# Where four small steps stand in a one-core layer kernel: bias split, cached values, row buffer clear, tile order of the last norm

## What is computed

```python
proj = x @ w_in                                   # 256 pool, 3x384 q k v, 768 conv columns
y_pool = pool_mix(u_pool)                         # causal means over 2, 4, 8, 16 rows, minus the row, times pool_w
y_attn = merge_dilations(branches)                # 6 heads x 64, windows (128,1), (512,4), (2048,16)
y_conv = silu(layer_norm(conv31(glu(c_in))))
x = layer_norm(alpha * x + concat(y_pool, y_attn, y_conv) @ w_o)      # first norm
# mixture of experts: 32 experts, top 4 per token
hh = xblk @ e_w_in[e] + e_b_in[e]
gate, up = clip(split(hh))
y = (gate * sigmoid(1.702 * gate) * (up + 1)) @ e_w_out[e] + e_b_out[e]
x = layer_norm(alpha * x + segment_sum(y * gate_of_token))            # final norm
```

## Time and profile before

| what | value |
|---|---|
| median of 3 runs | 1425.38 us (1423.78 to 1426.49) |
| the profiled execution's own time | 1424.93 us |
| its span in the profile | 1422.9 us |
| PE busy | 1228.7 us, 86% |
| DVE, ACT, GpSimd busy | 516.0, 176.7, 322.2 us |
| DMA moved | 463.12 MB, mean 325 GB/s |

### The profile page before, as it was taken

The page is one execution under the profiler, slowest core; times in us unless marked ns, Lnnn a source line. Parts: engine busy times, 40 slices in busy tenths (PEclk is TensorE's granted clock), DMA queues, the critical chain, the costliest instruction groups (busy, mean ns, idle before and its releaser), DMA issues.

```text
span 1422.9 us, 33256 instructions
## 1 busy us (share of the span) xinstructions
PE 1228.7 (86%) x12422; PEld 559.7 (39%) x12423; DVE 516.0 (36%) x822; ACT 176.7 (12%) x350; POOL 322.2 (23%) x266
## 2 busy tenths in 40 slices
PE   6996989996579999999989998998999889996860
PEld 5884454445123334345323343353343323442220
DVE  1996712347342224042222314042222222414225
ACT  0002312212010001011100101011000000101012
POOL 7103011314222121113312131123023212130113
PEclk9997968995689999999999999999999999998885
DMA  9600732026499999999999999999999999999973
GB/s 343 191 3 0 276 111 89 2 118 267 167 413 414 409 410 413 411 406 394 412 417 410 415 407 416 413 408 402 420 415 398 411 419 409 383 403 420 409 277 121
DMA packets 86539, 463.12 MB, mean 325 GB/s; under 512 B 13509, under 2 KB 29610, under 8 KB 36206
## 3 DMA queue, kind: packets, MB, share of 16 engines
q1 hardware_dynamic: 67483, 437.11, 75.5%
q0 software_dynamic: 16672, 18.27, 5.9%
q10 hardware_dynamic: 2354, 7.35, 1.4%
...
## 4 chain that ended last, share of the span: by engine, by line
PE 51%; DMA 17%; issue 3%; DVE 2%; SPq 1%; POOL 0%; POOLq 0%; ACT 0%; DVEq 0%; ACTq 0%
PE pu L1716 32%; PE rest L1730 17%; DMA ring<-in_e_in 9%; DMA ring<-in_e_out 7%; PE pu L1710 1%; SPq L267 1%; PE rest L1741 1%; DVE bn L1896 0%; DVE fin L1912 0%; DMA fin<-acc_rows 0%; DVE xgT L1836 0%; DVE mv L1906 0%; DMA acc_rows<-y,idx 0%; PE rest L1735 0%; DMA xq<-x_rows,idx 0%
## 5 line engine op out<-in xcount | busy, mean ns | idle before, releaser
L1716 PE MATMUL pu<-ring,xgT 128*32 128x512 f32 x5248 | 593.3, 606 | 32.3 <-DMA ring<-in_e_in 31.5
L1716 PEld LDWEIGHTS pu<-ring,xgT 128*32 128x32 f32 x5248 | 167.9, 111 | 440.3 <-issue 439.3
L1730 PE MATMUL rest<-ring,hid 128*32 128x256 f32 x5248 | 296.1, 381 | 19.9 <-DMA ring<-in_e_out 12.3
L1644 POOL DMA_INDIRECT acc_rows<-y,idx x82 | 130.2, 1588 | 758.0 <-ACT y L1784 729.0
L1866 DVE TENSOR_SCALAR gg<-pu 128x1280 f32<-128x1280 f32 x32 | 47.7, 1492 | 608.8 <-PE pu L1716 600.3
L1730 PEld LDWEIGHTS rest<-ring,hid 128*32 128x32 f32 x5248 | 173.2, 110 | 133.0 <-issue 36.1
L1776 ACT ACTIVATE ss<-gg 128x1280 f32<-128x1280 f32 x32 | 40.7, 1271 | 669.6 <-DVE gg L1866 669.6
L825 PE MATMUL pair<-xt,ring 128*128 128x260 f32 x448 | 100.6, 388 | 12.4 <-DMA ring<-in_w_in 12.4
L1635 POOL DMA_INDIRECT xq<-x_rows,idx x82 | 86.2, 1051 | 50.3 <-issue 45.5
L825 PEld LDWEIGHTS pair<-xt,ring 128*128 128x128 f32 x448 | 86.3, 193 | 25.6 <-DMA ring<-in_w_in 12.1
L1784 ACT ACTIVATE y<-rest,gate 128x256 f32 x160 | 61.9, 479 | 250.9 <-PE rest L1730 250.9
(11 more groups left out here) (260 smaller groups left out, 666.5 us busy)
## 6 DMA issues: line engine op xcount, KB each, us to landing
ring<-in_e_in SPq DMA_DIRECT2D x256, 1024.0 KB
ring<-in_e_out SPq DMA_DIRECT2D x128, 1024.0 KB
...
ring<-in_w_in SPq DMA_DIRECT2D x6, 512.0 KB, 12.1
...
```

The source lines that it names most:

```text
L1644: nc.gpsimd.indirect_dma_start(out=acc_quarters, out_offset=bass.IndirectOffsetOnAxis(ap=idx4[:, u % AHEAD, j:j + 1], axis=0), in_=y[:, u ...
L1716: mm = nc.tensor.matmul(pu[quarter(c), j], xgT[:, j, k], w[:, :, c * QC:(c + 1) * QC], start=False, stop=k == KT - 1, skip_group_check=True)
L1730: mm = nc.tensor.matmul(py[quarter(c), j], hid[:, j, 2 * q + f], w[:, f, c * QC:(c + 1) * QC], start=False, stop=q == FT // 2 - 1 and f == ...
```

## The change

Four edits, each of which puts work at another place or on another engine:

1. The out bias is no longer split by GpSimd ahead of the attention but behind its 24 scaling steps. Its rows are loaded by SyncE into the part of `qkv` that held the queries, once the last score product is done (`qk_done`), instead of by GpSimd into `btok`.
2. SyncE issues the cached values ahead of the last out weights and the two norm vectors.
3. GpSimd no longer clears `xq` ahead of the first gather. ACT clears half 0 (ones times zero), and the first gather waits for that; GpSimd clears half 1 between the gathers of jobs 0 and 1.
4. The final norm takes the tiles in the order 4, 0, 1, 2, 3. SyncE issues all five loads in that order. The addition of l2b for the last one (tile 3) is done by DVE.

```diff
@@ -66,6 +66,7 @@
...
 UNITS = 12
+LAST_TILES = (4, 0, 1, 2, 3)
 PAD0 = R + 4
...
@@ -543,23 +544,26 @@
...
             stepped(sp, f"v{NT}")
-            sp.dma_start(flat[:, wo0 + (NPART - 1) * D:wo0 + (KT - 1) * D].rearrange("p (k n) -> p k n", n=D), w_o[:, NPART:]
-                         ).then_inc(ld["wo2"], 16)
-            sp.dma_start(l1g, o["ln1_g"].partition_broadcast(P)).then_inc(ld["l1"], 16)
-            sp.dma_start(l1b, o["ln1_b"].partition_broadcast(P)).then_inc(ld["l1"], 16)
             sp.wait_ge(scored, 1)
...
                              ).then_inc(ld["vc"], 16)
+            sp.dma_start(flat[:, wo0 + (NPART - 1) * D:wo0 + (KT - 1) * D].rearrange("p (k n) -> p k n", n=D), w_o[:, NPART:]
+                         ).then_inc(ld["wo2"], 16)
+            sp.dma_start(l1g, o["ln1_g"].partition_broadcast(P)).then_inc(ld["l1"], 16)
+            sp.dma_start(l1b, o["ln1_b"].partition_broadcast(P)).then_inc(ld["l1"], 16)
             sp.wait_ge(sn_done, 1)
...
                 load_unit(sp, 0, j)
+            sp.wait_ge(qk_done, nsteps)
+            for part in range(3):
+                sp.dma_start(qkv[part * NE:(part + 1) * NE, 0:D], o["e_bout"][0]).then_inc(ld["bout"], 16)
             stepped(sp, "pv2")
...
@@ -609,23 +613,6 @@
...
             keep_high(2 * NE, 3 * NE)
-            for part in range(3):
-                gp.dma_start(btok[part * NE:(part + 1) * NE, 0:D], o["e_bout"][0]).then_inc(ld["bout"], 16)
-            sp_ch.do(nc.gpsimd.memset(drow[:, :], 0.0))
-            gp.wait_ge(ld["bout"], 48)
-            gp.wait_ge(conv_done, 1)
-            def keep_high_out(lo, hi):
-                sp_ch.do(nc.gpsimd.tensor_copy(drow[lo:hi], btok[lo:hi, 0:D]))
-            def take_off_out(lo, hi):
-                sp_ch.do(nc.gpsimd.tensor_tensor(btok[lo:hi, 0:D], btok[lo:hi, 0:D], drow[lo:hi], ALU.subtract))
-            keep_high_out(0, 3 * NE)
-            for part in (1, 2):
-                take_off_out(part * NE, (part + 1) * NE)
-                keep_high_out(part * NE, (part + 1) * NE)
-            take_off_out(2 * NE, 3 * NE)
-            keep_high_out(2 * NE, 3 * NE)
             gp.sem_inc(brow_ready, 1)
...
@@ -648,6 +635,22 @@
...
                     list_rows(NT, 1)
+            otok = qkv[:, 0:D]
+            gp.wait_ge(ld["bout"], 48)
+            gp.wait_ge(listed, 16 * TOPK)
+            def keep_high_out(lo, hi):
+                sp_ch.do(nc.gpsimd.tensor_copy(drow[lo:hi], otok[lo:hi]))
+            def take_off_out(lo, hi):
+                sp_ch.do(nc.gpsimd.tensor_tensor(otok[lo:hi], otok[lo:hi], drow[lo:hi], ALU.subtract))
+            sp_ch.do(nc.gpsimd.memset(drow[:, :], 0.0))
+            keep_high_out(0, 3 * NE)
+            for part in (1, 2):
+                take_off_out(part * NE, (part + 1) * NE)
+                keep_high_out(part * NE, (part + 1) * NE)
+            take_off_out(2 * NE, 3 * NE)
+            keep_high_out(2 * NE, 3 * NE)
             for i in range(NT):
...
@@ -1603,18 +1608,19 @@
...
             sp.wait_ge(sums_done, 1)
-            for i in (0, 2, 4):
+            for i in LAST_TILES:
                 load_sums(sp, i)
-            for i in range(NT + 1):
-                sp.wait_ge(y_ready, i + 1)
+            for n, i in enumerate(LAST_TILES):
+                if n < NT:
+                    sp.wait_ge(y_ready, n + 1)
+                else:
+                    sp.wait_ge(last_ready, 1)
                 dst = o["y_prompt"][0, i * P:(i + 1) * P] if i < NT else o["y_sample"][:, 0]
...
         def _(gp):
-            nc.gpsimd.memset(xq[:, :, :, :], 0.0).then_inc(xq_zero, 1)
-            gp.wait_ge(xq_zero, 1)
 
...
@@ -1651,6 +1657,11 @@
...
                 gp.wait_ge(named, u + 1)
+                if u == 0:
+                    gp.wait_ge(xq_zero, 1)
+                if u == 1:
+                    nc.gpsimd.memset(xq[:, 1], 0.0).then_inc(xq_half_zero, 1)
+                    gp.wait_ge(xq_half_zero, 1)
                 if u >= 1:
...
@@ -1686,9 +1697,9 @@
...
             gp.sem_inc(sums_done, 1)
-            for i in range(NT + 1):
+            for n, i in enumerate(LAST_TILES[:-1]):
                 m = rows(i)
-                gp.wait_ge(scaled2, i + 1)
+                gp.wait_ge(scaled2, n + 1)
                 nc.gpsimd.tensor_tensor(fin[0:m, i], fin[0:m, i], l2b[0:m], ALU.add).then_inc(y_ready, 1)
...
@@ -1785,6 +1796,9 @@
...
 
+            nc.scalar.activation(xq[:, 0].rearrange("p j n -> p (j n)").rearrange("p (a n) -> p a n", n=P),
+                                 C("ones").unsqueeze(1).broadcast_to([P, JG * QC // P, P]), ACT.Copy, scale=0.0
+                                 ).then_inc(xq_zero, 1)
             a.sem_inc(y_done, 2)
...
@@ -1796,20 +1810,19 @@
...
 
-            def ln2_root(i):
-                a.wait_ge(var2, i + 1)
+            def ln2_root(n):
+                i = LAST_TILES[n]
+                a.wait_ge(var2, n + 1)
                 nc.scalar.activation(mv2[0:rows(i), i, 3:4], mv2[0:rows(i), i, 1:2], ACT.Sqrt).then_inc(rstd2, 1)
-            a.wait_ge(sums_done, 1)
-            for i in (1, 3):
-                load_sums(a, i)
-            for i in range(NT + 2):
-                if i <= NT:
-                    ln2_root(i)
-                if i >= 1:
-                    m = rows(i - 1)
-                    a.wait_ge(shift2, i)
-                    nc.scalar.activation(fin[0:m, i - 1], fin[0:m, i - 1], ACT.Identity, bias=mv2[0:m, i - 1, 4:5],
-                                         scale=mv2[0:m, i - 1, 2:3]).then_inc(normed2, 1)
+            for n in range(NT + 2):
+                if n <= NT:
+                    ln2_root(n)
+                if n >= 1:
+                    i = LAST_TILES[n - 1]
+                    m = rows(i)
+                    a.wait_ge(shift2, n)
+                    nc.scalar.activation(fin[0:m, i], fin[0:m, i], ACT.Identity, bias=mv2[0:m, i, 4:5],
+                                         scale=mv2[0:m, i, 2:3]).then_inc(normed2, 1)
 
...
@@ -1889,35 +1902,41 @@
...
 
-            def moments(i):
+            def moments(n):
+                i = LAST_TILES[n]
                 m = rows(i)
...
                 for h in range(2):
-                    fc.mark(V.bn_stats(bn2[0:m, i % 2, h], fin[0:m, i, h * 512:(h + 1) * 512]))
+                    fc.mark(V.bn_stats(bn2[0:m, n % 2, h], fin[0:m, i, h * 512:(h + 1) * 512]))
                 fc.wait()
-                fc.do(V.bn_aggr(mv2[0:m, i, 0:2], bn2[0:m, i % 2].rearrange("p h s -> p (h s)")))
+                fc.do(V.bn_aggr(mv2[0:m, i, 0:2], bn2[0:m, n % 2].rearrange("p h s -> p (h s)")))
                 V.tensor_scalar(mv2[0:m, i, 1:2], mv2[0:m, i, 1:2], EPS / ALPHA_N ** 2, None, ALU.add).then_inc(var2, 1)
 
-            def shift(i):
+            def shift(n):
+                i = LAST_TILES[n]
                 m = rows(i)
-                d.wait_ge(rstd2, i + 1)
+                d.wait_ge(rstd2, n + 1)
                 fc.do(V.reciprocal(mv2[0:m, i, 2:3], mv2[0:m, i, 3:4]))
...
 
-            def scale(i):
+            def scale(n):
+                i = LAST_TILES[n]
                 m = rows(i)
-                d.wait_ge(normed2, i + 1)
+                d.wait_ge(normed2, n + 1)
                 V.tensor_tensor(fin[0:m, i], fin[0:m, i], l2g[0:m], ALU.mult).then_inc(scaled2, 1)
 
-            for i in range(NT + 3):
-                if i <= NT:
-                    moments(i)
-                if 1 <= i <= NT + 1:
-                    shift(i - 1)
-                if i >= 2:
-                    scale(i - 2)
+            for n in range(NT + 3):
+                if n <= NT:
+                    moments(n)
+                if 1 <= n <= NT + 1:
+                    shift(n - 1)
+                if n >= 2:
+                    scale(n - 2)
+            i = LAST_TILES[NT]
+            d.wait_ge(scaled2, NT + 1)
+            V.tensor_tensor(fin[0:rows(i), i], fin[0:rows(i), i], l2b[0:rows(i)], ALU.add).then_inc(last_ready, 1)
 
...
```

2 lines of the change are left out of this document (added).

## The result

The changed kernel takes **1401.15 us** (median of 4 runs, 1400.63 to 1404.66) beside 1425.35 us for the kernel before in the same series (1423.78 to 1426.49): a ratio of 0.9839, 95% interval 0.9827 to 0.9851, or 24.2 us less. The prediction was 1403.2 us in a range of 1393 to 1413. The profiled execution took 1400.86 us, of which the span is 1398.8.

What follows compares the result with a forecast made beforehand. Bound taken: an expert-weight stream started by the first job, after a dependent PE, DVE and ACT chain. 9.8 + 8.0 + 2.2 + 2.4 - 0.3 = 22.1 us saved gives 1403.2 us, range 1393 to 1413.

Steps and rivals of the forecast that it cites:

- the forecast case: Whole kernel: the shifts of all four edits come through and sum to 22.1 us, giving 1403.2 us; chance 0.75.
- The DVE part: Pooling mixer: DVE's sums no longer wait out GpSimd's split rows, and all 8.3 us saved reach PE's first product.
- The step that was open: PE clock at the pooling mixer: 1.0 us from the first product and 0.5 of 2.8 from the variance product.
- Its price at the new place: Split behind the attention: it may hold up DVE's first norm, 0 to 1.5 us, taken as 0.3.
- alone, the values are 3.1/5.7 of it, 11.5 us: Cached values ahead of the out weights: landing time shared by bytes, near 183 us, so PE's 5.1 us wait goes.
- The fear for DVE's naming rows: Row buffer: clearing the other half, about 1.1 us, may block DVE's row-naming copies; saving 1.1 to 2.2 us.
- so 1.2 us more: End of the final norm: the last store, 512 KB in place of 32 KB, costs 1.2 us more at 411 GB/s.
- The first rival: Pooling sums: DVE's long rows come from their own odd shapes, not GpSimd; 9.8 us becomes 0, 1413.1 us; chance 0.04.
- The second: Cached values land no faster alone, the queue's own rate counts; their move gives 1.3 us, total 1410.0 us; chance 0.09.
- The third: Pooling mixer and sample values: both clocks stay up once the waits are gone; 32.0 us saved, 1393.3 us; chance 0.08.
- The fourth: Expert stream: PE work meets lower clock phases, mean down by 0.025, ending 2.9 us slower at 1428.3 us; chance 0.02.
- The fifth: Whole kernel: the stream swallows all shifts and nothing shows within 0.2%; chance 0.02.

Runs made afterwards that it cites:

- the one with 18 products of no use: Kernel before, with eighteen useless PE products in the 9.27 us gap ahead of the first pooling product: 1422.95 us, ratio 0.9986.
- the kernel with the idle casts: Changed kernel, with GpSimd casts and subtractions put back at the split's old place, their result unread: 1415.93 us, 0.9917 of the kernel before.

## Why the prediction was right, term by term

The sum was 22.1 us and the profiled span is 24.1 shorter; the forecast case is the one that came. The mechanisms of all four edits were right, three sizes were not, and that the sum came so near is in part luck.

**Edit 1, front: 9.8 predicted, 12.4 in the profiled run.** The DVE part is right: from the sum of squares (109.46 and 110.10) to the first pooling product there were 19.15 us and are 10.37, 8.8 us less for my 8.3, and the wait that stays is 0.49 us for the 1 us I counted. Most of the half us is the additions: they follow by 0.60 us, where I took 0.72. One reading was loose: only the four small copies of the stretch of the earlier trace rows end with a GpSimd row (within 0.03 us). The three stretched additions end 0.55 us behind one, as if they waited for it and then ran. The step that was open is the clock. I counted 1.5 us; from the first product to the v projection it took 3.6 us less in this execution, 2.0 in the two with a variance product of 4.50 and 4.55, and 1.0 in the two with 5.54. From the sum of squares to the v projection the edit gives 12.4, 10.7 to 10.8 or 9.7 us, all against the one profile of before, with its 5.54 (the kernel with edit 2 alone, whose front is that of before, had 4.85). My 9.8 is what it gives when the clock falls again over the variance product; 12.4 lies just above my bound of 12.1.

**Its price at the new place: 0.3 predicted, nothing found.** The bias rows were there in time (2.6 us from issue to landing), DVE was idle for 14.89 us beside the split, and it is shorter than I took it, 11.9 us with its clear and not about 15: without DVE beside it a cast takes 1.03 and not up to 1.86 us, a subtraction 2.12 and not 2.44. I had taken durations from a place where the two engines block each other.

**Edit 2: 8.0 predicted, 5.6 in the changed kernel's trace, 5.7 in the trace with this edit alone.** The two sizes missed in one direction. The wait: 5.1 us counted, 4.6 gone (4.8 in the kernel with this edit alone). The failed step is "alone, the values are 3.1/5.7 of it, 11.5 us", which shares the time by bytes; they took 16.4 us, 14.4 when nothing is behind them. The error of 4.9 us was larger than the slack of 4.4 us (11.5 us from 171.27 is 182.8, and PE wanted them at 187.17), and cost only the last 0.5 us. The clock: 2.9 us counted for the first group, 1.0 gone (6.99 to 5.97). I had read the fall at 217 us with PE busy rightly and then still given the group nearly all of the upper level; in eight profiles with a wait of at most 0.65 us the group took 4.97 to 6.62 us, so 0.4 to 2.0 us came back, and the 2.9 lie above all of them.

**Edit 3: 2.2 predicted, 1.8 in the changed kernel's trace and 2.0 in the times alone.** ACT's clear took the 1.27 us of the row I named; the gather is issued 0.9 us behind its end and not 0.45, 2.19 us behind the block's start where I had named 2 as the sign. I had put the old 1.79 us to the reading of the job's size alone; DVE's first naming row, for which the gather waits too, took 1.74 us beside the old clear, to its very end, and takes 0.22 beside ACT's. The fear for DVE's naming rows came true (1.27 for 0.22 us) and cost nothing.

**Edit 4: 2.4 predicted, 3.7 measured, above my upper bound of 2.6.** The earlier start (2.4 counted, 2.64 measured) and the addition (1.2 counted, 1.16 in the kernel that puts it back) are right. The failed step is the last store: "so 1.2 us more" for 512 KB in place of 32. The span ends 3.0 us after the last addition in both kernels (1422.9 - 1419.88 and 1398.8 - 1395.79), and over all profiles 2.97 to 3.02 us with the small store and 3.01 to 3.09 with the large one. So the larger store costs 0.1 us at most; I had taken the stream's rate for a cost on top, with no row for it.

**The stream and the rivals.** First product to last: 1010.8 and 1009.9 us, well within the 3 us that I named. No wait for out weights appears, and the list rows wait for DVE alone. The measured terms give 12.4 + 5.6 + 1.8 + 3.7 = 23.5 us, less 0.6 at the start, and 1.2 more by no term of mine, most of it between the first group of sample values and the first norm (the shift grows from 17.3 to 18.45 us there). That is no work of an edit but the clock of the attention: from the third group to the row of 308.56 it is 93.75 us before and 92.32 after, and 90.79 to 94.05 over the fourteen profiles, in no order of the edits. Ten products of the out projection (L950), for example, took 6.11 us at 245.20 in the kernel before and 4.56 in the one with 18 products of no use, whose program is the same there.

The sum of 22.1 was near because 2.4 us too much on edit 2 and 0.4 on edit 3 stood against 2.6 too little on edit 1, 1.3 on edit 4 and the 0.3 of the price.

The first rival (DVE's rows are its own) is excluded by the kernel with the idle casts. The second (no faster alone) is excluded in its full form, but its reason, the values' own rate, was what the term was missing. The third had half a point: the clock can stay up at the front, never over the whole first group of sample values. The fourth (the stream at a lower clock) did not come: from 373 to 1380 us the granted clock is 0.98, 0.99 and 0.96 by thirds before, 0.98, 0.99 and 0.95 after. The fifth is out by the shift of 20.99 us at the stream's end.

**What stays open:** what makes DVE stand still in the routing, and why it is long in one execution and short or absent in others. In both long ones a packet of an instruction queue (q14) falls into it, 6 to 7 us ahead of its end, and in the short ones none, but such packets stand at the same step in the profiles without a standstill too. The four without one are also the four of one series. Open is further what decides the clock over the variance product.
